# Expert values in a PEER layer: every fourth gathered row scaled on ScalarE and summed on GpSimd, with the activations held in PSUM

## The reference, cut to what matters

```python
def peer_ffn(xn, wq, keys1, keys2, u_tab, v_tab):
    ...                      # top-16 of product keys per head -> expert, gate
    def block(args):
        xb, eb, gb = args
        ub = u_tab[eb]
        vb = v_tab[eb]
        act = jax.nn.gelu(jnp.einsum('td,thkd->thk', xb, ub), approximate=False)
        return jnp.einsum('thk,thkd->td', gb * act, vb)
```

## Time and profile before

| | |
|---|---|
| median of 3 runs | 4342.82 us (4341.18 to 4344.03) |
| the profiled execution's own time | 4336.71 us |
| its span, first to last instruction | 4334.8 us |
| TensorE matmul busy | 3589.7 us (83%) |
| VectorE busy | 2684.7 us (62%) |
| ScalarE busy | 1564.1 us (36%) |
| GpSimd busy | 1536.3 us (35%) |
| moved by the GpSimd gather queue | 1342.26 MB |

### The profile page before, as it was taken

The page is one execution under the profiler, slowest core; times in us unless marked ns, Lnnn a source line. Parts: engine busy times, 40 slices in busy tenths (PEclk is TensorE's granted clock), DMA queues, the critical chain, the costliest instruction groups (busy, mean ns, idle before and its releaser), DMA issues. The chain is left out here.

```text
span 4334.8 us, 33292 instructions
## 1 busy us (share of the span) xinstructions
PE 3589.7 (83%) x10024; PEld 1674.6 (39%) x10024; DVE 2684.7 (62%) x6235; ACT 1564.1 (36%) x4522; POOL 1536.3 (35%) x1338
## 2 busy tenths in 40 slices
PE   8899989778778778779777768997877877877776
PEld 1289563233233223223222227785332322322222
DVE  2221349785875875875875445664987587587444
ACT  1121014344334334334333332552444433433333
POOL 0101304444444444444444321000454444444442
PEclk9899599999999999999999999998999999999999
DMA  8712029999999999999999982003999999999998
GB/s 309 267 59 88 0 109 421 403 421 421 421 419 421 415 410 422 416 415 420 414 415 422 421 359 72 4 1 132 421 400 421 421 421 420 420 409 415 422 421 338
DMA packets 232988, 1455.27 MB, mean 336 GB/s; under 512 B 25140, under 2 KB 25140, under 8 KB 67812
## 3 DMA queue, kind: packets, MB, share of 16 engines
q0 software_dynamic: 184320, 1342.26, 74.7%
q1 hardware_dynamic: 48392, 110.79, 7.2%
q10 hardware_dynamic: 96, 0.10, 0.0%
HBM read 1447.72 MB, written 5.34 MB: 335 GB/s over the span
## 5 line engine op out<-in xcount | busy, mean ns | idle before, releaser
L1345 PE MATMUL peer_py<-peer_ring,peer_diag 128*128 128x512 f32 x5120 | 2505.0, 625 | 620.8 <-ACT peer_diag L1275 610.1
L1445 DVE CUSTOM_DVE_ANT_0 peer_ring<-peer_ring,peer_f 128x1024 f32<-128x1024 f32 x1280 | 1556.1, 1224 | 918.6 <-DMA peer_ring<-in_uv_dram,peer_idx 909.9
L1228 POOL DMA_INDIRECT peer_ring<-in_uv_dram,peer_idx x1280 | 1451.7, 1134 | 1817.9 <-PE peer_py L1345 1692.5
L1345 PEld LDWEIGHTS peer_py<-peer_ring,peer_diag 128*128 128x128 f32 x5120 | 929.3, 194 | 2148.7 <-ACT peer_diag L1275 1320.4
L1269 ACT ACTIVATE peer_gel<-peer_u 128x1 f32<-128x1 f32 x1280 | 258.8, 202 | 1827.0 <-DVE peer_u L1445 1825.7
L1275 ACT ACTIVATE peer_diag<-ident,peer_coef 128x128 f32<-128x128 f32 x1280 | 513.8, 401 | 41.7
L1273 ACT ACTIVATE peer_coef<-peer_gel,peer_gate 128x1 f32<-128x1 f32 x1280 | 377.1, 295 | 46.7 <-ACT peer_gel L1269 0.4
L316 DVE TENSOR_TENSOR m_w_low<-m_w_low_plain,m_w_high 128x2048 fp32r<-128x2048 f32 x26 | 61.0, 2347 | 218.1 <-ACT m_w_high L311 218.1
L1219 POOL IOTA peer_iota<- 128x16 f32 x2 | 0.3, 144 | 502.1 <-POOLq L763 361.3
L324 PE MATMUL m_ps<-m_w_high,m_aT_high 128*128 128x512 f32 x416 | 165.5, 398 | 3.3 <-DVE m_v L748 1.6
L1320 PE MATMUL peer_pb<-arena,peer_fT 128*128 128x512 f32 x320 | 164.6, 612 | 2.4 <-ACT peer_fT L1242 2.4
(11 more groups left out here) (189 smaller groups left out, 2732.3 us busy)
## 6 DMA issues: line engine op xcount, KB each, us to landing
arena<-in_ada_w_dram SPq DMA_DIRECT2D x16, 2048.0 KB, 10.3
peer_ring<-in_uv_dram,peer_idx POOLq DMA_INDIRECT x1280, 14.9
mod_rows_sb<-in_ada_w_dram SPq DMA_DIRECT2D x8, 2048.0 KB, 10.3
m_w_low_plain<-in_ev_w_in_dram SPq DMA_DIRECT2D x12, 1024.0 KB, 5.0
arena<-in_peer_wq_dram SPq DMA_DIRECT2D x2, 4096.0 KB, 18.4
mod_rows_sb<-mod_rows SPq DMA_DIRECT2D x7, 1024.0 KB, 7.1
m_w_low_plain<-in_od_w_in_dram SPq DMA_DIRECT2D x6, 1024.0 KB, 5.3
m_w_low_plain<-in_ev_w_out_dram SPq DMA_DIRECT2D x4, 1024.0 KB, 5.0
```

The source lines that it names most:

```text
L1228: pool.indirect_dma_start(ring[:, n % RING], None, A["uv"], bass.IndirectOffsetOnAxis(idx[:, i % 2, hd, k:k + 1], 0)).then_inc(sem(f"lande ...
L1345: ins = pe.matmul(PY[:, i % 2, b], diag[:, n % RING], ring[:, n % RING, D + b * HALF:D + (b + 1) * HALF], start=s == 0, stop=s == TS - 1)
L1445: dve.tensor_tensor_reduce(x, x, f[:, i % 2], 1.0, 0.0, ALU.mult, ALU.add, u[:, n % RING:n % RING + 1]).then_inc(sem("dot"), 1)
```

## The change

`aside(n)` names the slots with n % 4 = 3. For these ScalarE no longer writes a diagonal: it scales the v half in its ring buffer in place by the coefficient (1024 columns), and GpSimd adds the result to a sum in SBUF, `beside` (the first of a tile is copied there). TensorE skips them, so it has 96 slots a tile. GpSimd does such an addition right before it issues the gather that takes over that buffer. The activations move: VectorE writes them to `fn` in SBUF, TensorE transposes from there, and ScalarE copies them to `f` in PSUM at the start of each tile (`settle`), which `dot` then reads. PY shrinks to one half, and TensorE waits before slot 0 of each tile but the first until `add_up` of the tile before has read PY. `add_up` adds `beside` to PY before it multiplies by the gate row.

```diff
+ASIDE = 4
+def aside(n):
+    return n % ASIDE == ASIDE - 1
+def on_pe(n):
+    return n - n // ASIDE
...
-        f = sb("f", [P, 2, D])
+        fn = sb("f", [P, D])
+        beside = sb("beside", [P, 2, D])
...
-        PY = ctx.enter_context(nc.psum_tensor(f"peer{layer}_py", [P, 2, 2, HALF], F32))
+        PY = ctx.enter_context(nc.psum_tensor(f"peer{layer}_py", [P, 2, HALF], F32))
+        f = ctx.enter_context(nc.psum_tensor(f"peer{layer}_f_ps", [P, D], F32))
...
+            def add_beside(n):
+                i, s = divmod(n, TS)
+                v, acc = ring[:, n % RING, D:2 * D], beside[:, i % 2]
+                pool.wait_ge(sem("scaled"), n // ASIDE + 1)
+                if s == ASIDE - 1:
+                    if i >= first + 2:
+                        pool.wait_ge(sem("y"), i - 1)
+                    pool.tensor_copy(acc, v).then_inc(sem("beside"), 1)
+                else:
+                    pool.wait_ge(sem("beside"), n // ASIDE)
+                    pool.tensor_tensor(acc, acc, v, ALU.add).then_inc(sem("beside"), 1)
...
-                    if n >= RING:
-                        pool.wait_ge(sem("slot_free"), n - RING + 1)
+                    if n - RING >= first * TS and aside(n - RING):
+                        add_beside(n - RING)
+                        pool.wait_ge(sem("beside"), (n - RING) // ASIDE + 1)
+                    elif n - RING >= first * TS:
+                        pool.wait_ge(sem("slot_free"), on_pe(n - RING + 1))
...
+            for n in range((last + 1) * TS - RING, (last + 1) * TS):
+                if aside(n):
+                    add_beside(n)
...
-                act.activation(diag[:, n % RING], ident[:], ACT.Copy, scale=coef[:, at]).then_inc(sem("diag"), 1)
+                if aside(n):
+                    v = ring[:, n % RING, D:2 * D]
+                    act.activation(v, v, ACT.Copy, scale=coef[:, at]).then_inc(sem("scaled"), 1)
+                else:
+                    act.activation(diag[:, n % RING], ident[:], ACT.Copy, scale=coef[:, at]).then_inc(sem("diag"), 1)
+            def settle(i):
+                act.wait_ge(sem("fn"), i + 1)
+                act.wait_ge(sem("dot"), i * TS)
+                act.activation(f[:], fn[:], ACT.Copy).then_inc(sem("f"), 1)
...
             def combine(i, s):
                 n = i * TS + s
-                if s == 0 and i >= 2:
-                    pe.wait_ge(sem("y"), i - 1)
-                pe.wait_ge(sem("diag"), n + 1)
+                if aside(n):
+                    return
+                if s == 0 and i >= 1:
+                    pe.wait_ge(sem("y"), i)
+                pe.wait_ge(sem("diag"), on_pe(n + 1))
...
             def modulate(i):
-                x = f[:, i % 2]
+                x = fn[:]
+                if i > first:
+                    dve.wait_ge(sem("f"), i)
...
             def dot(i, s):
+                if s == 0:
+                    dve.wait_ge(sem("f"), i + 1)
...
             def add_up(i):
-                dve.wait_ge(sem("slot_free"), (i + 1) * TS)
+                dve.wait_ge(sem("slot_free"), on_pe((i + 1) * TS))
+                dve.wait_ge(sem("beside"), (i + 1) * TS // ASIDE)
...
-                dve.tensor_tensor(y[:], PY[:, i % 2].rearrange("p b n -> p (b n)"), rows[:, kind(i - shift), 2], ALU.mult).then_inc(sem("y"), 1)
+                dve.tensor_tensor(y[:], PY[:].rearrange("p b n -> p (b n)"), beside[:, i % 2], ALU.add).then_inc(sem("y"), 1)
                 dve.wait_ge(sem("y"), i + 1)
+                link(dve.tensor_tensor(y[:], y[:], rows[:, kind(i - shift), 2], ALU.mult))
                 link(dve.tensor_tensor(h[:, i - shift], h[:, i - shift], y[:], ALU.add))
```

More of the change, by code:

```diff
@@ L1285, in _ @@
             for i in range(first, last + 1):
+                settle(i)
                 for s in range(TS):
@@ L1309, in f_transposes @@
             def f_transposes(i):
-                pe.wait_ge(sem("f"), i + 1)
+                pe.wait_ge(sem("fn"), i + 1)
                 if i > 0:
@@ L1313, in f_transposes @@
                 for k in range(KC):
-                    ins = pe.transpose(PB[:, k // 4, (k % 4) * P:(k % 4 + 1) * P], f[:, i % 2, k * P:(k + 1) * P], ident[:])
+                    ins = pe.transpose(PB[:, k // 4, (k % 4) * P:(k % 4 + 1) * P], fn[:, k * P:(k + 1) * P], ident[:])
                 ins.then_inc(sem("fT_ps"), 1)
@@ L1340, in combine @@
                 n = i * TS + s
-                if s == 0 and i >= 2:
-                    pe.wait_ge(sem("y"), i - 1)
-                pe.wait_ge(sem("diag"), n + 1)
+                if aside(n):
[3 more added lines that the diff above has]
+                pe.wait_ge(sem("diag"), on_pe(n + 1))
                 for b in range(2):
-                    ins = pe.matmul(PY[:, i % 2, b], diag[:, n % RING], ring[:, n % RING, D + b * HALF:D + (b + 1) * HALF],
-                                    start=s == 0, stop=s == TS - 1)
+                    ins = pe.matmul(PY[:, b], diag[:, n % RING], ring[:, n % RING, D + b * HALF:D + (b + 1) * HALF],
+                                    start=s == 0, stop=s == TS - 2)
                 ins.then_inc(sem("slot_free"), 1)
@@ L1387, in modulate @@
             def modulate(i):
-                x = f[:, i % 2]
+                x = fn[:]
                 dve.wait_ge(sem("root"), i + 1)
+                if i > first:
+                    dve.wait_ge(sem("f"), i)
                 link(dve.reciprocal(ss[:, 3:4], ss[:, 2:3]))
                 link(dve.scalar_tensor_tensor(x, h[:, i - shift], ss[:, 3:4], rows[:, kind(i - shift), 1], ALU.mult, ALU.mult))
-                dve.tensor_tensor(x, x, rows[:, kind(i - shift), 0], ALU.add).then_inc(sem("f"), 1)
-                dve.wait_ge(sem("f"), i + 1)
+                dve.tensor_tensor(x, x, rows[:, kind(i - shift), 0], ALU.add).then_inc(sem("fn"), 1)
+                dve.wait_ge(sem("fn"), i + 1)
             def top16(out, where, values):
@@ L1442, in dot @@
                 n = i * TS + s
+                if s == 0:
+                    dve.wait_ge(sem("f"), i + 1)
                 dve.wait_ge(sem(f"landed{n % RING}"), 16 * (n // RING + 1))
                 x = ring[:, n % RING, 0:D]
-                dve.tensor_tensor_reduce(x, x, f[:, i % 2], 1.0, 0.0, ALU.mult, ALU.add, u[:, n % RING:n % RING + 1]).then_inc(sem("dot"), 1)
+                dve.tensor_tensor_reduce(x, x, f[:], 1.0, 0.0, ALU.mult, ALU.add, u[:, n % RING:n % RING + 1]).then_inc(sem("dot"), 1)
             def add_up(i):
-                dve.wait_ge(sem("slot_free"), (i + 1) * TS)
+                dve.wait_ge(sem("slot_free"), on_pe((i + 1) * TS))
+                dve.wait_ge(sem("beside"), (i + 1) * TS // ASIDE)
                 if i == first:
                     dve.wait_ge(S("peer_gates"), 16 * rows_loads)
-                dve.tensor_tensor(y[:], PY[:, i % 2].rearrange("p b n -> p (b n)"), rows[:, kind(i - shift), 2], ALU.mult).then_inc(sem("y"), 1)
+                dve.tensor_tensor(y[:], PY[:].rearrange("p b n -> p (b n)"), beside[:, i % 2], ALU.add).then_inc(sem("y"), 1)
                 dve.wait_ge(sem("y"), i + 1)
+                link(dve.tensor_tensor(y[:], y[:], rows[:, kind(i - shift), 2], ALU.mult))
                 link(dve.tensor_tensor(h[:, i - shift], h[:, i - shift], y[:], ALU.add))
```

## The result

The change costs time. The kernel with it takes 4374.56 us in the median of 4 runs (4368.65 to 4379.21), the kernel before 4343.42 us in 4 runs beside them (4341.18 to 4344.82): ratio 1.0071, 95% interval 1.0054 to 1.0089, 31.1 us more. The profiled execution took 4379.21 us and lies 4.7 us above its median, where the one of before lies 6.7 us under; so 11.4 us of the 42.6 between the two spans are chance of these executions.

The account below looks back on a forecast made before the run. DMA transfers were taken to bound the kernel; 17 us at boundaries, 5 at stage ends and 3 in first tiles make 25 us, 4336.7 to 4361.7, plus 6.1 us to the runs' median: 4368 us, range 4346 to 4396.

Parts of the forecast that it names:

- What bounds the kernel: PEER stages: DMA transfers at 2.49 us a slot are the bound, so a quarter less on TensorE gains 0 us.
- An aside slot's way: Aside slots: buffers come free about 1.1 us later, leads fall to some 13 us, hidden: 0 us.
- rival C: Aside slots: pauses keep TensorE at 1.2 GHz and it becomes the bound; about 4483 us, chance 0.06.
- f in PSUM: Dots and tile starts: dots stay as long, `settle` is hidden by slot 2: 0 us.
- One PY: Tile boundaries: TensorE's wait delays the gather of (i, 8); 2.1 us at each of 8 boundaries, +17 us.
- the lower clock holds for the second slot as well: Tile boundaries: TensorE's second slot also slow, another 0.9 us lost, of which half was added.
- The ends: Ends of both stages: scaling, GpSimd's addition and one more VectorE operation add 2.4 us, twice: +5 us.
- The first tiles: Each stage's first tile: GpSimd's additions hold VectorE's two-SBUF-input routing operations, 7 us against 5.1 us of idle: +3 us.
- Rival D: First tiles: every head's routing meets two additions and VectorE becomes the bound; 4388 us, chance 0.13.
- Rival B: Tile boundaries: the lead covers the wait if (i, 8) is issued by T + 14.4; 4349 us, chance 0.18.
- Rival E: First tiles: the starved stretch after the first tile's stall closes and boundaries cost nothing; faster, 4333 us, chance 0.06.

Follow-up runs that it names:

- early_inner: The changed kernel with `add_up` behind slot 1's dot, and each stage's first tile and last four aside slots all on TensorE: 4347.37 us, ratio 1.0017.
- warm: The changed kernel with 14 matmuls that nothing reads on TensorE ahead of its wait at each of 8 tile boundaries: 4366.52 us, ratio 1.005.
- early_r1: The changed kernel with `add_up` behind the dot of slot 1 in place of 4, and aside slots at n % 4 = 1: 4374.96 us, ratio 1.0078.
- aside_sbuf: The changed kernel with the aside slots alone: f in SBUF, PY in two halves, no `settle`: 4405.2 us, ratio 1.0155.
- early_add: The changed kernel with `add_up` called behind the dot of slot 1 in place of 4: 4355.97 us, ratio 1.0036.
- before_s48: The kernel before, with ScalarE's copy of the second half of the next tile's scores at slot 48 instead of 42: 4334.2 us, ratio 0.9984.

## Why the prediction was right, and where its steps failed

**What bounds the kernel.** Right. A quarter less on TensorE is worth nothing, which early_inner shows without the change's losses: 0.17% slower than before.

**An aside slot's way, costed at 0.** Right in its sizes: ScalarE's scaling takes 1148 ns (1.15 forecast), GpSimd's addition 2357 ns in the median, and leads fell to 13.3 and 13.1 us (13 forecast), far from 5.4. The granted clock did fall with the pauses (0.87 in the mean of the second window above, 1.00 in the earlier trace rows), and the DMA share stayed 1.01: **rival C** is refuted. The rule that the forecast set beside it, from the Trainium skill, page TensorE: Matmul & The Clock Gate, section "HAM oscillation — how this bites in real kernels", agrees with the trace in the clock; a price in time it has only where TensorE is waited for, the 8.0 us of warm at the boundaries and the 0.9 us at the end of early_r1.

**f in PSUM, costed at 0.** The dots took 1.22 us, and `settle` held the first dot of tile 2 until 1307.39, T + 1.2 (T + 1.6 forecast; VectorE sat idle for 2.69 us there, some 1.2 of which it has before any dot), made good by slot 2, as forecast. I had seen in it a cost and not what it buys: aside_sbuf is 31 us slower than the change.

**One PY: 2.1 us a boundary, 17 us.** The total is nearly right (18.6 by early_add; 26 less 6 in the profile), and the place is right: TensorE resumes after 12.44 us of idle at a clock of 0.50, the issue of (i, 8) comes at T + 16.4 (T + 16.0 forecast), with a lead of 5.3 to 5.6 us at seven boundaries and 6.8 at one (5.45 forecast), and (i, 8) is 2.2 us late (1.6 forecast). What failed is the term behind it, the 0.5 us for "the lower clock holds for the second slot as well": at five of the eight boundaries (i, 9) is issued 1.72 us behind (i, 8), the pace of full clock. What costs there is 1.6 us, it is paid at every boundary, and warm shows that it comes at full clock as well: the gathers' own restart. It could have been read beside the earlier trace rows: 780.83 is the landing behind the stall, and in the trace of before the next one came at 784.24, 3.4 us later, not 2.49:

```profile
784.24 1.23 DVE L1445 CUSTOM_DVE_ANT_0 peer_ring<-peer_ring,peer_f 128x1024 f32<-128x1024 f32 x1 [2.18 <-DMA peer_ring<-in_uv_dram,peer_idx]
```

That the total came out near is in this part luck. Some 0.6 us of a boundary's 3.9 are in the kernel before as well, and the tiles behind a starved boundary lose 0.7 us less in their inner slots; why they do, no run here tells.

**The ends: 5 us.** 2.45 us in PEER 0, as forecast (9.8 against 7.3). In PEER 1 it is 5.6 us, the same in every kernel whose last slot is an aside slot: the step that failed is that only the chain from the dot to VectorE's last operation was counted. VectorE ends 2.5 us later there too, but the next stage starts when all engines have closed their part, and GpSimd closes late. Its closing instruction, which the timeline view leaves out and the trace holds, takes 4.59 us in PEER 0 (from 2605.88) and 9.65 us in PEER 1 (from 4353.26), so until 4362.9, just ahead of 4363.17. It starts with the last addition, whose 2.34 us it includes. In early_r1 it begins 1.9 us ahead of the last dot, takes as long, and is over before VectorE's last operation starts. In the kernel before it is longer still, 16.55 and 19.11 us, but starts at the last gather's issue, some 15 us ahead of the last dot, and is over before the sum is. I had costed GpSimd's work and not its closing. Why it is 5 us longer in PEER 1 was not tried.

**The first tiles: 3 us.** 7.4 us in the profile, 3.7 to 6.0 by the two pairs of runs. The waiting itself was sized nearly right: 7 us were forecast for six heads, and 5.7 and 5.8 us stand in the traces up to slot 46. Two steps failed. One is which operations can meet an addition: I took those with two SBUF inputs alone, and all three that were held there in PEER 0, and all three in PEER 1, have one input (they are TENSOR_SCALAR operations of 16 numbers, some 170 ns before and up to 3.04 us here). The Trainium skill, page SBUF — State Buffer, section "SBUF: two separate sides", names beside the VectorE operations with two SBUF inputs also those in a 2-port performance mode as ones that take the shared pair; I had left that half of its sentence out. The trace agrees in that operations with one input were held; in which mode they ran, no run here shows. The other step is the room: I set 5.1 us of idle against the waiting, and by slot 46 the tiles had lost 2.8 and 3.7 us against the kernel before, so only 2 to 3 us of it were made good. That the waiting came out near 7 us is chance, since the forecast took the meetings as chance at any phase ("about one in two heads meets one"), and early_r1, two slots away, has 14.9 us of it.

**Rival D** did not come true for the change, but VectorE did become the bound of the first tiles in aside_sbuf and early_r1 (4405 and 4375 us), so the change stands near that edge. **Rival B** fell with the issue of (i, 8) at T + 16.4, where it needed T + 14.4; in warm, at T + 14.8, (i, 8) is only 0.45 us late. **Rival E** is refuted for the change; but its stall exists, and before_s48 takes it away, for 8.5 us by the medians (6.9 by the ratio), without any of the change.

Taken together: the forecast was 4368 us, slower, in a range of 4346 to 4396, and 4374.6 were measured. Its 25 us stand against 31.1: 17 against 18.6, 5 against 8, 3 against 4 to 6. The path it named carries most of the loss; the restart of the gathers, GpSimd's closing and the one-input operations were not in it.
